# Opening projections in parts with transposes one tile ahead, masks built early, and z units between output transposes

## The reference, cut to what matters

```
xn = _rmsnorm(h, norm_g)
proj = jnp.einsum("bld,de->ble", xn, w_in)
v_c, g_c, z_c, u_s, z_s, gl_c, gl_s = _split_columns(proj)
y_c = _conformer_conv(v_c, g_c, z_c, dw_w, dw_b, ln_g, ln_b)   # ends: silu(layernorm) * silu(z_c)
y_s = _s5_scan(u_s, lam_re, lam_im, log_step, b_re, b_im, c_re, c_im, d_skip)
y_s = jax.nn.gelu(y_s)
y_s = y_s * jax.nn.sigmoid(jnp.einsum("ble,ef->blf", y_s, w_glu) + b_glu)
y_s = y_s * jax.nn.silu(z_s)
merged = gate_c * (y_c @ w_conv) + gate_s * (y_s @ w_ssm)      # gates: sigmoid(gl + b)
h = h + jnp.einsum("bld,de->ble", merged, w_out)
out = _rmsnorm(h, final_g)
```

## Time and profile before

| what | value |
|---|---|
| time, median of 3 runs | 1682.09 us (1681.53 to 1707.98) |
| the profiled execution's own time | 1683.64 us |
| its span on the slowest core (core 2) | 1682.1 us |
| spans of the 8 cores | 1675.6 to 1682.1 us |
| mean granted TensorE clock of the cores | 0.993 to 0.997 |
| PE busy | 1625.8 us (97%), 9088 instructions |
| DVE busy | 729.9 us (43%) |
| ACT busy | 515.0 us (31%) |
| POOL busy | 62.6 us (4%) |
| chain that ended last | PE 89%, ACT 4%, DVE 3%, issue 2%, DMA 1% |

### The profile page before, as it was taken

How to read it: one execution, slowest core, us unless ns; L and a number is a source line. 1 busy time by engine, 2 the same in 40 slices (tenths; PEclk the granted TensorE clock), 3 DMA queues, 4 the chain that set the end, 5 groups by cost and what they waited for, 6 DMA issues and landing times.

```text
span 1682.1 us, 23373 instructions; the slowest of 8 cores (1675.6 to 1682.1 us)
## 1 busy us (share of the span) xinstructions
PE 1625.8 (97%) x9088; PEld 796.6 (47%) x9262; DVE 729.9 (43%) x1124; ACT 515.0 (31%) x751; POOL 62.6 (4%) x133
## 2 busy tenths in 40 slices
PE   5899999999999999999999999999999999999998
PEld 3444555555554444455554444444444444444443
DVE  4572788878840003565625211111112347543333
ACT  4663577777742110013322511111111000021111
POOL 1000000000000001000000000000000000000000
PEclk9999999999999999999999999999999999999999
DMA  9822132322349224982232203022221435454443
GB/s 220 235 67 50 30 85 57 74 66 57 76 87 177 50 39 55 113 116 37 51 70 38 51 13 63 0 38 38 39 38 38 150 118 193 164 164 150 150 154 122
DMA packets 33470, 148.61 MB, mean 88 GB/s; under 512 B 3969, under 2 KB 7169, under 8 KB 24193
## 3 DMA queue, kind: packets, MB, share of 16 engines
q0 software_dynamic: 13456, 58.20, 22.1%
q1 hardware_dynamic: 19906, 88.91, 15.4%
HBM read 178.03 MB, written 40.89 MB: 130 GB/s over the span
## 4 chain that ended last, share of the span: by engine, by line
PE 89%; ACT 4%; DVE 3%; issue 2%; DMA 1%; POOL 0%; DVEq 0%; ACTq 0%; POOLq 0%; SPq 0%
PE ps L257 87%; PE ps L276 2%; ACT cs L229 1%; DVE xs L245 1%; DMA xt<-x 1%; ACT xs L231 1%; ACT L229 1%; ACT yc L229 0%; DVE pt L235 0%; ACT wv L229 0%; ACT gst L229 0%; ACT tt L229 0%; PE ps L260 0%; DVE h L245 0%; DVE smp L235 0%
## 5 line engine op out<-in xcount | busy, mean ns | idle before, releaser
L257 PE MATMUL ps<-xm,wr 128*128 128x512 bf16 x1236 | 289.2, 379 | 3.7 <-ACT gst L229 1.6
L257 PE MATMUL ps<-wb,xm 128*128 128x512 bf16 x998 | 222.6, 381 | 1.8 <-issue 0.6
L257 PE MATMUL ps<-xm,zr 128*128 128x512 bf16 x1000 | 221.1, 379 | 1.3
L257 PE MATMUL ps<-wo,m 128*128 128x512 bf16 x1004 | 220.1, 379 | 1.1
L257 PEld LDWEIGHTS ps<-xm,wr 128*128 128x128 bf16 x1280 | 119.8, 98 | 129.5 <-issue 4.9
L257 PE MATMUL ps<-xm,gr 128*128 128x512 bf16 x752 | 168.7, 379 | 0.8
L257 PEld LDWEIGHTS ps<-wo,m 128*128 128x128 bf16 x1024 | 100.2, 98 | 120.8
L257 PEld LDWEIGHTS ps<-xm,zr 128*128 128x128 bf16 x1024 | 99.7, 98 | 118.2
L257 PEld LDWEIGHTS ps<-wb,xm 128*128 128x128 bf16 x1024 | 99.7, 98 | 118.3 <-issue 2.2
L231 ACT ACTIVATE jk<-h 128x2048 bf16<-128x2048 f32 (+1 forms) x19 | 31.2, 1641 | 324.8 <-DVE h L245 324.8
L257 PE MATMUL ps<-wu,xm 128*128 128x512 bf16 x496 | 117.9, 393 | 9.1 <-ACT wv L229 2.4
(11 more groups left out here) (171 smaller groups left out, 1706.5 us busy)
## 6 DMA issues: line engine op xcount, KB each, us to landing
xt<-x SPq DMA_DIRECT2D x16, 1024.0 KB, 9.5
x<-x SPq DMA_DIRECT2D x16, 1024.0 KB, 6.9
out<-h SPq DMA_DIRECT2D x15, 1024.0 KB, 4.8
wr<-wm POOLq DMA_DIRECT2D x20, 512.0 KB, 6.9
gscr<-gst SPq DMA_DIRECT2D x20, 512.0 KB, 6.7
gr<-gscr SPq DMA_DIRECT2D x20, 512.0 KB, 3.6
wob<-wo POOLq DMA_DIRECT2D x8, 1024.0 KB, 23.3
zr<-wm POOLq DMA_DIRECT2D x16, 512.0 KB, 5.6
```

The lines of the kernel that those rows point to most:

```text
L257: return S.op("pe", lambda e: e.matmul(out_, lhsT, rhs, start=start, stop=stop), r, w, signal=signal)
```

## The change

1. **Masks.** `consts()` gets a scratch of its own (IOS, 1024 columns) with a separate place for each iota, so that POOL writes all of them in a row. It is recorded ahead of the two copies of GF instead of behind them.
2. **x load.** The load of position 2 no longer waits for position 0 to land.
3. **Order.** A can be recorded in parts of four k. The first three A run in four parts each, mixed by part; T(i) now stands directly in front of A(i), where A(i-1) stood between them; N(i+3) follows T(i+1). The B steps begin after A12, and eight of them (B9 to B16) stand behind A16, where four did.
4. **Second-half weights.** Loaded behind positions 6, 8, 10 and 11.
5. **umeta** moves from behind B7 to behind A15.
6. **z units.** Behind block b (b > 0) of the output transposes the four units of one z projection are recorded; the last of the eight follows the loop.

```diff
+        IOS = T("ios", [128, 1024], F32, D0 + 94208)
...
-        ev_x[2] = load_x(2, (ev_x[0],))
+        ev_x[2] = load_x(2)
...
+        consts()
         cp("act", GF.ap[:, 0:1024], ps2[0], r=(PB[0], PB[1]), a=(GFb,))
         cp("dve", GF.ap[:, 1024:2048], ps2[1], r=(PB[2], PB[3]), a=(GFb,))
...
-        def uproj(i, nb):
+        def uproj(i, nb, k0=0, k1=16):
...
-            for k in range(16):
+            for k in range(k0, k1):
                 mm(ps[bk], xmt(t, k), WU[nb].ap[:, k, :], k == 0, k == 15,
                    r=(XMB[t], WUB[nb][k // 4]), w=(PB[bk],), signal=(k == 15))
+            if k1 < 16:
+                return
...
-        load_wu(1, 0, (ev_x[3],))
...
-        order = ["T0", "N2", "T1", "N3"]
-        b_after = {8: 1, 9: 1, 10: 2, 11: 2, 12: 2, 13: 2, 14: 1, 15: 2}
+        order = ["T0", "N2", "A0:0", "A0:1", "T1", "N3", "A1:0", "A1:1", "A0:2", "A1:2", "T2", "N4", "A2:0", "A2:1",
+                 "A2:2", "A0:3", "A1:3", "A2:3", "T3", "N5", "A3", "T4", "N6"]
+        b_after = {12: 2, 13: 2, 14: 3, 15: 2}
         nbu = 0
-        for i in range(NSEQ):
+        for i in range(4, NSEQ):
             order += [f"A{i}"]
             for _ in range(b_after.get(i, 0)):
                 order += [f"B{nbu}"]
                 nbu += 1
-            if i + 2 < NSEQ:
-                order += [f"T{i + 2}"]
-            if i + 4 < NSEQ:
-                order += [f"N{i + 4}"]
+            if i + 1 < NSEQ:
+                order += [f"T{i + 1}"]
+            if i + 3 < NSEQ:
+                order += [f"N{i + 3}"]
...
-                if i + 3 in (5, 7, 9):
-                    load_wu(1, (i + 3 - 3) // 2, (ev_x[i + 3],))
+                if i + 3 in (6, 8, 10, 11):
+                    load_wu(1, (6, 8, 10, 11).index(i + 3), (ev_x[i + 3],))
...
                 if i == NSEQ - 2:
+                    umeta()
                     prep_wt(0)
                     tab_a(0)
...
-                if i == 7:
-                    umeta()
...
             fillg(1)
+            if b > 0:
+                zc_m(7 + b)
         for _ in gen:
             pass
+        zc_m(15)
```

More of the change, by code:

```diff
@@ L353, in build, with scratch, iota @@
         WUs = [[dsrc() for _ in range(4)] for _ in range(2)]
[L356 to L359, removed]
+        IOS = T("ios", [128, 1024], F32, D0 + 94208)
+        ioff = [0]
+        def scratch(n):
+            o = ioff[0]
+            ioff[0] += n
+            assert ioff[0] <= 1024
+            return IOS.ap[:, o:o + n], IOS.buf(4 * o, 4 * o + 4 * n)
+        def iota(ap, pat, base, cm, b):
+            S.op("pool", lambda e: e.iota(ap, pat, base=base, channel_multiplier=cm,
+                                          allow_small_or_imprecise_dtypes=True), w=(b,))
+        io0, io0b = scratch(240)
+        iota(io0, [[1, 240]], 0, -1, io0b)
+        ts(IDP.ap, io0, 0.0, None, ALU.is_equal, r=(io0b,), w=(IDPb,))
         seq = list(range(6)) + ["m"] + list(range(6, NTILE))
@@ L435, in build @@
         ub = [0]
-        def uproj(i, nb):
+        ubank = {}
+        def uproj(i, nb, k0=0, k1=16):
             t = seq[i]
-            bk = 4 + ub[0] % 4
-            ub[0] += 1
+            if k0 == 0:
+                ubank[i, nb] = 4 + ub[0] % 4
+                ub[0] += 1
+            bk = ubank[i, nb]
             if t == "m":
@@ L469, in build @@
         assert D0 + 94208 + 3584 + 512 <= TOP
[L471 to L505, removed]
         def params():
@@ L825, in btr @@
                w=(YSB[b][2 * par], YSB[b][2 * par + 1]))
-        consts()
         par = params()
@@ L1305, in load_mw, with load_w4, zc_m @@
             return s
[L1307 to L1310, removed]
-                if i < 10:
-                    load_z(i + 4)
-                elif 12 <= i < 14:
-                    load_z(i + 2)
-                if i >= 11 and len(w4) < 2:
-                    j = len(w4)
-                    w4.append([load_gw(16 + j), load_gw(32 + j), load_mw(wcv_d[j]), load_mw(wss_d[j])])
         w4 = []
-        zc_phase()
-        while len(w4) < 2:
+        def load_w4():
             j = len(w4)
             w4.append([load_gw(16 + j), load_gw(32 + j), load_mw(wcv_d[j]), load_mw(wss_d[j])])
+        def zc_m(i):
+            for n in range(4):
+                z_unit(i, n, YC, YCB)
+            if i < 10:
+                load_z(i + 4)
+            elif 12 <= i < 14:
+                load_z(i + 2)
+            if i >= 11 and len(w4) < 2:
+                load_w4()
+        for b in range(8):
+            hs = [yc_tr(b, h) for h in range(2)]
+            for h, (pT, bk) in enumerate(hs):
+                act(YC.ap[:, b, h * 1024:(h + 1) * 1024], pT, AF.Silu, bias=PRM.ap[:, PR_LNB + b:PR_LNB + b + 1],
+                    scale=PRM.ap[:, PR_LNG + b:PR_LNG + b + 1], r=(PB[bk], PRMb),
+                    w=(YCB[b][2 * h], YCB[b][2 * h + 1]))
+            fillg(1)
+            if b > 0:
+                zc_m(7 + b)
+        for _ in gen:
+            pass
+        zc_m(15)
+        while len(w4) < 2:
+            load_w4()
         def pmm(w_, wb_, src, srcB, n, bk):
```

52 lines of the change are left out of this document (42 added, 10 removed).

## The result

The changed kernel takes 1714.0 us (median; 1713.5 to 1714.3), against 1682.1 before: ratio 1.0191, 95% interval 1.0161 to 1.0220. That it is slower is certain; whether by 2% is open, since the interval holds 1.02. The forecast was 1711.4 within 1688 to 1728. In some executions half of the chip runs at a lower clock and takes longer; the times in this part are medians of the others, except the 1682.1 (1681.8 without its one slow execution), while some recorded expectations name medians over all, up to 0.8 us higher. The profiled execution takes 1714.3 us, with spans of 1707.6 to 1712.7 us on the 8 cores; the change lies on all of them alike.

A forecast was written before the change was run, and what follows sets the result against it. PE was taken as the bound. The first gate matmul comes 34.8 us later, less 5.5 for z units: +29.3 on the profiled 1683.6 is 1712.9, or 1711.4 on the median (range 1688 to 1728).

The forecast's parts named there:

- the rival that ended on the fast side: Opening: tiles flow without an open copy, early first transpose and z units gain in full; 1672 us, chance 0.08.
- the 6.1: Start of the opening: early masks bring the first transpose 6.1 us earlier, to 15.5.
- Parts of A: From T0 to A3: PE waits for x tiles and their copies; 29.5 us with 13.9 of work, 15.6 lost.
- T directly before its A: Each tile's copy latency of 1.4 us lies open, 5.75 us a tile; 6.7 lost A3 to A7, 5.6 at last four.
- Params: A7 to A12: PE's copies stand behind params work on DVE and ACT; 45.7 us with 21.7 of work, 24.0 lost.
- The rival by which they hide (1689): A7 to A12: DVE does the params while PE works, loss falls from 24.0 to 7; 1689 us, chance 0.17.
- Low clock: A7 to A12: A behind long waits runs at 1.2 GHz, 1.8 us more each, four not hidden; 7 lost.
- The rival by which the clock falls at 1.4 us: Nearly every tile: waits of 1.4 us also bring the low clock, some nine more A; 1727 us, chance 0.17.
- umeta, preparations: Before the first gate matmul: `ut` wait falls from 2.4 to 0.4; `wv` and `ug` waits and low clock stay; 5.5 lost.

The follow-up runs named there:

- b2: Kernel before with only the masks built early, by the new `consts()` in its new place; 1.001 of the kernel before (1684.7 us).
- a2: Changed kernel with no params steps behind A7 to A11, four behind each A from A12 on, `bct` loads moved too; 1700.8 us.
- a1: Changed kernel with T again two positions ahead of its A from position 3 on; 1699.8 us.
- a7: Changed kernel with B steps as early as before, each between T(i+1) and A(i+1), and second-half weights loaded as before; 1693.0 us.
- a5: Changed kernel with the second-half weights loaded at their places of before; 1715.0 us, 1.0192 of the kernel before.
- b1: Kernel before with only the z units put between the output transposes; 1677.7 us, 0.9971 of the kernel before.
- b5: Kernel before with the z units between the output transposes and umeta behind A15; 1674.1 us, 0.9947 of the kernel before.
- b8: Kernel before with early masks and the x load of position 3 held until the last quarter of the first weights landed; 1687.5 us.

## Why the prediction was right, point by point

The working gave a start for each step, and these are the measured ones.

| step | forecast | measured | stretch before it, forecast and measured |
|---|---|---|---|
| T0 | 15.5 | 14.17 | |
| A3 | 45.0 | 47.86 | 29.5, 33.7 |
| A7 | 66.3 | 69.44 | 21.3, 21.6 |
| A8 | 73.8 | 78.82 | 7.5, 9.4 |
| A9 | 83.85 | 88.59 | 10.05, 9.8 |
| A10 | 95.0 | 102.63 | 11.15, 14.0 |
| A11 | 105.4 | 113.10 | 10.4, 10.5 |
| A12 | 112.0 | 119.84 | 6.6, 6.7 |
| first gate matmul | 209.8 | 210.86 | 97.8 with 7.0 of low clock, 91.0 |

**Masks.** The start was nearly right (1.3 us better than forecast; the 17 operations run from 6.02 to 9.2, 3.1 us and not 4.5). That it is worth something was wrong: b2 gives -6.9 us at T0 and +1.4 at the gate. In the sum this did no harm, since the 15.6 us up to A3 were worked out from the landing of x, but the rival that ended on the fast side counted the 6.1 as sure, and no kernel here has them.

**Parts of A.** Forecast 15.6 lost up to A3, measured 19.8. The landing of tile 3 (31.66 for 31) and the start of A2 (37.53 for 37.5) were right. Missing was the low clock of the 24 matmuls behind the wait of 5.5 us: T3 follows them at 45.55, 8.02 us behind their start, where 5.2 stood in the sum. That is 2.8 of the 4.2; 1.3 is the better T0, which the landing of x turned into waiting.

**T directly before its A.** Right, to 0.02 us: A3 stands 2.31 behind its T, which is 0.89 and 1.42; a2 has the tiles 5.76 apart where 5.75 was worked out. The prediction held this part "to decide"; a1, which takes it back from A3 on and leaves the params and the late B steps, wins 15.2 of the 35.9 us. At the last four tiles the waits are 1.25, 1.25, 1.53 and 1.25 us. A3 to A7 lost 7.0 (6.7).

**Params.** Right in place and in size: the stretches that hold them alone are within 0.3 us (A8 to A9, A10 to A11, A11 to A12), and A9's end to A10 took 7.7 us (94.96 to 102.63), as the terms give. Without its params (a2) A7 to A12 is 19.9 us shorter; a1 shows that the distance of two tiles does not hide them either, a7 that B work hides most of them. The rival by which they hide (1689) is out. In the changed kernel's ACT rows a function starts 1.30 us behind the start of its table load (95.83 and 97.13), and the load 0.01 us behind the end of the operation before it (95.22 + 0.60). The Trainium skill (ScalarE: Activation LUTs, What ACT_TABLE_LOAD costs) counts 2.66 us to a switch with its drain; this trace disagrees, as it did before the change.

**Low clock.** Right in its total, and that by luck. The 1.8 us for an A at the low clock set a row's duration (5.30) against a distance from start to start (3.45); from start to start it is 5.14, 1.7 more. Forecast were four such A on the path, A7, A9, A11 and A12, 7 us. On the path of the slowest core are A7 (+1.7) and A9 (+2.9); A11 and A12 ran at the high level. A10's +2.7 delays A11 no more than the DVE chain does, as the working said, and the +2.8 of the mixed A's were not foreseen. The sum is 7.4 for 7, out of other pieces. The granted clock of A8 and A9, behind waits of 3.18 and 5.27 us, as a share of 2.4 GHz (the third value from the end):

```profile
78.82:82.27 3.45, 3.45 (x16) 1.56 (x17) 0.69 (x2) 2.47 (x4) 0.00 (x0) 1.00 1.02 278
88.59:94.96 6.37, 6.37 (x17) 2.22 (x17) 5.33 (x4) 0.00 (x0) 0.00 (x0) 0.53 0.39 132
```

A8 ran at 2.4 GHz throughout, A9 nearly all the way at 1.2. On cores 1, 3 and 7 it was the other way round: A8 took 5.30 us, which the DVE chain hides, the wait for A9 was 3.58, and A9 took 3.61. These cores reach the gate at 205.6 to 205.9, the cores 2, 4 and 5 with the slow A9 at 209.6 to 210.9. The rival by which the clock falls at 1.4 us is out: behind all six waits of 1.25 us and both of 1.53 the A ran at the high level, 3.61 us for 16 matmuls or 10.52 for 48. The Trainium skill (TensorE: Matmul & The Clock Gate, HAM oscillation) tells of bursts that each start at the low clock behind waits of some 3 to 5 us; the waits of 1.4 that the rival is about are shorter, and here a wait of 3.2 left either level.

**umeta, preparations.** Forecast 5.5 lost with the last tiles' 5.6; from A12 to the gate 11.4 us were lost against 11.1. The low clock behind the wait of 2.42 is there (179.44 to 184.58, 1.7 us).

**Second-half weights.** Nothing, as forecast (a5).

**z units.** Gain 5.5 forecast, 5.3 in the changed kernel and 5.2 alone (b1). In the kernel before PE waited at eight of the twelve groups of transposes, 4.0 us in all.

**The sum.** It was 2.6 us under the measured median. 1.3 are terms: -1.3 at T0, +4.2 up to A3, +0.3 up to A7, -2.3 from A7 to A12 (28.7 lost, 31.0 with the low clock charged there), +0.2 up to the gate and +0.2 for the z units. The other 1.3 lie in the step from one execution to the median: the profiled one of before was 1.55 above its median, that of after 0.3. The mechanism and place of the losses to waits were those of the working. The mis-sized term is the stretch up to A3, and the low clock fell in other places than forecast.

## What to carry to other kernels

An operation of PE that is set directly behind the one whose evacuation it needs opens the latency of that evacuation at every tile, and everything else on the evacuating engines' lists along with it: here 1.4 us a tile by itself, but 20 us more in five tiles where small vector work stood in the same list. Filler work (the B steps) was worth most where the other engines were late: moving six of the B steps there gave some 20 us back. An early start of compute is worth nothing while the loads are the bound. Here it was worth a little less than nothing (b2), because it let another load in earlier.

## What the runs showed of the hardware that was not expected

- **Wait length alone does not set the clock.** The same B stands behind the same wait of 2.42 us on every core of these kernels. It took 5.25 to 5.30 us on all 8 cores before the change and 3.61 on all 8 of a2; in the changed kernel it was 5.30 on five cores and 3.61 on three, in b5 four and four. Behind 3.18 and 3.24 us A8 and A11 took 3.61 on the slowest core of the changed kernel, while 3.16 in a7 and 3.30 in a1 gave 5.30. The longest, 6.53 and 6.34 us, stood behind 5.27 and 6.62. What else decides was not settled.
- **A transfer issued earlier can delay another queue's.** The last weights quarter released PE at 31.5 us in the kernel before, at 34.1 with the early masks (b2) and at 29.6 with an x load held back (b8). On the cores it scatters by 1 to 3 us within a kernel, but the three kinds of opening overlap little.
- **Two PSUM banks moved gave about as much as the z units,** the largest gain among the parts of the change: 4.5 us in the mean of the cores (4.9 by the mean spans of all executions, 1669.9 and 1665.0), out of 3.4 us of waits that the waits view showed already before the change and, on half of the cores, 1.7 of low clock behind the first of them.
